# Sixteen of the 44 activation tiles of the last projection move from triple products into seven block products per pair, between its passes

## The chip, the cores and the metric

The kernel runs on one core of a Trainium2 chip. The metric is the device time of one execution in microseconds (us). TensorE (PE) multiplies, VectorE (DVE) and ScalarE (ACT) prepare and take away operands, GpSimd (POOL) and SyncE (SP) issue most of the transfers.

## What is computed

One layer of a hybrid block on 512 tokens of 2048 channels. A mixer with a modulated norm comes first, then a SwiGLU feed-forward of width 5632 and a final norm. The end is what the change is about:

```python
def _swiglu(u, w_ffn_in, w_ffn_out):
    gate, up = jnp.split(u @ w_ffn_in, 2, axis=-1)
    return (jax.nn.silu(gate) * up) @ w_ffn_out
...
        x = x + g2 * _swiglu(_modulate(_rms_norm(x, norm2_g[l]), sh2, sc2), w_ffn_in[l], w_ffn_out[l])
...
    return _rms_norm(x, norm_f_g)
```

`g2` is the last sixth of a modulation vector, `silu(c) @ w_ada + b_ada`.

## The kernel before

Everything is in fp32. Each operand is split into a high part (ACT copies it into a rounded type) and a low part (DVE subtracts), and a product is three matmuls: high by high, high by low, low by high. There is no scheduler: each engine has its program written out by hand, with counted semaphores between them, so the order within a program is fixed.

Two ways of multiplying are in use. **Triples:** a unit of 4 activation tiles (128 channels each) by 2 output tiles is 24 matmuls of 512 columns. **Block products** (`period`): for a pair of output tiles, 16 activation tiles are halved in channels and tokens, and seven half-size products (`ORDER`) with sums of weight blocks (`gate_sums`, `w_sums`) take the place of eight. Each product is 8 matmuls of 512 columns and 8 of 256. 24 periods make the merge gates, 40 make most of the feed-forward's input (`NALL` counts 64 in all). The results of the seven are combined by ACT and DVE in `up_out`, `c12_out`, `up_fold` and `gate_out`.

The last projection multiplies the 44 tiles of the hidden activation, kept in DRAM, by `w_ffn_out`. It has three passes over the activation, for output tiles 0 to 5, 6 to 11 and 12 to 15. A pass has 11 groups of 4 activation tiles, and a group has 3, 3 or 2 units. Two sets of buffers alternate: group n is loaded by SP when group n-2 has been multiplied (`b_used`), then ACT makes its high parts and DVE its low parts (`prep`: one tile `hb` of 2048 columns, and per unit one tile `bw` of 1024). At the end of a pass DVE takes the sums out of the accumulators with `down_out`, which multiplies by `g2` and adds to the rows `x1b` of the residual, and counts `b_free`. The first units of the next pass wait for `b_free`, since they write the same accumulators. ACT squares these rows and prepares them for transposing (`squares_out`), TensorE transposes them (`turn`), and `fin_evac` copies the result.

The modulation is computed on the side: chunks of `w_ada` (512 KB, 1024 columns) are loaded by POOL into a ring and added up on DVE (`chunk`, 1024 columns); then TensorE sums over partitions by one-column matmuls (`spread`). 16 chunks are added while the first projection's last 8 units run (u from 8 to 15), 64 during later stages, and the last 16, of twice the width, beside pass 0 (`chunks_late`). Their spread, of 16 columns, stands in the last group of pass 0.

## Time and profile before

| | us |
|---|---|
| median of 3 runs | 2650.99 (2649.25 to 2652.12) |
| the profiled execution, its own time | 2649.97 |
| its span from the first to the last instruction | 2648.2 |
| TensorE busy | 2609.0 (99%) |
| VectorE busy | 1891.1 (71%) |
| ScalarE busy | 1157.8 (44%) |
| last projection, first matmul | 2138.76 after the start |
| its first matmul of pass 1 / pass 2 | about 2322 / 2502 to 2508, where the passes change |

Times of places are counted from the start of the span. Busy shares say which engine has no room. Of a pipelined TensorE the distance between the starts of matmuls is the price, not the length of one. 1.8 us of the execution lie outside the span.

### The profile page before, as it was taken

What the parts mean: (1) busy time and instruction counts of PE and PEld (TensorE: products, weight loads), DVE (VectorE), ACT (ScalarE), POOL (GpSimd) and SP (SyncE); (2) the same over time, 40 slices, a digit from 0 to 9 for tenths busy, and PEclk for the clock granted to TensorE, in tenths of its full rate; (3) what the DMA queues carried; (4) which work ended last, traced back from release to release, by engine and by line L of the source; (5) the groups of instructions that cost most, each with busy time, mean ns of one, the idle gap of its engine ahead of it and who ended that gap; (6) DMA issues with size and microseconds to landing.
All of it is one profiled execution on the core that took longest, in us unless ns stands there. A gap on an engine that the chain in (4) does not pass through costs nothing.

```text
span 2648.2 us, 37757 instructions
## 1 busy us (share of the span) xinstructions
PE 2609.0 (99%) x13881; PEld 2204.5 (83%) x13881; DVE 1891.1 (71%) x2070; ACT 1157.8 (44%) x1311; POOL 175.4 (7%) x242
## 2 busy tenths in 40 slices
PE   6999999999999999999999999999999999999998
PEld 4788778878888888888788888888888888888887
DVE  4546898767999999775767878878788756533443
ACT  4214766354555555322444444444444433333333
POOL 0010000000001111110000001000010000000000
PEclk8999999999999999999999999999999999999999
DMA  9963434755556665985568888888888757644555
GB/s 369 369 198 117 137 120 147 266 175 168 162 160 168 154 163 144 330 319 193 151 160 209 202 198 203 193 210 201 195 207 196 194 207 285 246 151 158 175 178 187
DMA packets 505787, 527.43 MB, mean 199 GB/s; under 512 B 16041, under 2 KB 445937, under 8 KB 497905
## 3 DMA queue, kind: packets, MB, share of 16 engines
q1 hardware_dynamic: 464064, 388.35, 47.4%
q0 software_dynamic: 37088, 121.13, 19.0%
q10 hardware_dynamic: 4560, 16.95, 1.6%
q8 instruction: 49, 0.80, 0.1%
q14 instruction: 26, 0.21, 0.0%
HBM read 435.65 MB, written 48.76 MB: 183 GB/s over the span
## 4 chain that ended last, share of the span: by engine, by line
PE 94%; DVE 2%; ACT 1%; DMA 1%; issue 0%; ACTq 0%; DVEq 0%; SPq 0%
PE main L1549 15%; PE aux L1549 15%; PE main L1257 8%; PE main L1553 8%; PE aux L1553 8%; PE main L1258 8%; PE main L1259 8%; PE aux L1687 4%; PE aux L1688 4%; PE aux L1689 4%; PE main L1688 2%; PE main L1689 2%; PE main L1687 2%; PE aux L1432 1%; PE aux L1309 1%; DMA ada_pc<-in_w_ada 1%
## 5 line engine op out<-in xcount | busy, mean ns | idle before, releaser
L939 ACT ACTIVATE h_S<-f_S 128x1024 fp32r<-128x1024 f32 x256 | 264.2, 1057 | 385.5 <-DVE f_S L2123 186.9
L2135 DVE TENSOR_TENSOR l_S<-f_S,h_S 128x1024 fp32r<-128x1024 f32 x256 | 306.3, 1218 | 13.2 <-ACT h_S L939 13.2
L2135 DVE TENSOR_TENSOR l_A<-f_A,h_A 128x1024 fp32r<-128x1024 f32 x192 | 232.1, 1221 | 67.0 <-ACT h_A L939 56.0
L939 ACT ACTIVATE h_A<-f_A 128x1024 fp32r<-128x1024 f32 x192 | 202.3, 1057 | 133.9 <-PE aux L1553 66.0
L1810 DVE TENSOR_TENSOR w_lo<-w_raw,w_hi 128x1024 fp32r<-128x1024 f32 x120 | 145.9, 1221 | 116.6 <-ACT w_hi L733 116.3
L1257 PE MATMUL main<-u_both,w_hi 128*128 128x512 f32 x512 | 210.9, 412 | 2.5 <-DVE u_both L2330 2.5
L2420 DVE TENSOR_TENSOR hb_l<-hb_f,hb_h 128x2048 fp32r<-128x2048 f32 x33 | 75.6, 2292 | 187.4 <-ACT hb_h L1165 187.4
L733 ACT ACTIVATE w_hi<-w_raw 128x1024 fp32r<-128x1024 f32 x120 | 125.7, 1053 | 179.7 <-DMA w_raw<-in_w_out 69.5
L1687 PE MATMUL aux<-hb_h,bw_h 128*128 128x512 f32 x512 | 201.5, 394 | 0.9 <-DVE bw_l L2425 0.9
L1258 PE MATMUL main<-u_both,w_hi 128*128 128x512 f32 x512 | 201.6, 394 | 0.0
L1259 PE MATMUL main<-u_both,w_lo 128*128 128x512 f32 x512 | 200.5, 392 | 0.0
L1688 PE MATMUL aux<-hb_l,bw_h 128*128 128x512 f32 x512 | 200.3, 391 | 0.0
L1689 PE MATMUL aux<-hb_h,bw_l 128*128 128x512 f32 x512 | 200.3, 391 | 0.0
L1549 PE MATMUL main<-t_both,h_S 128*128 128x512 f32 x768 | 192.3, 392 | 0.0
L1549 PE MATMUL aux<-t_both,h_S 128*128 128x512 f32 x768 | 192.3, 392 | 0.0
L1165 ACT ACTIVATE hb_h<-hb_f 128x2048 fp32r<-128x2048 f32 x33 | 63.2, 1916 | 221.6 <-DMA hb_f<-hidden_feature_major 207.6
L1549 PEld LDWEIGHTS main<-t_both,h_S 128*128 128x128 f32 x768 | 138.2, 189 | 24.7
L1549 PEld LDWEIGHTS aux<-t_both,h_S 128*128 128x128 f32 x768 | 138.1, 189 | 24.7
L1549 PE MATMUL main<-u_both,h_A 128*128 128x512 f32 x512 | 128.2, 392 | 0.0
L1549 PE MATMUL aux<-u_both,h_A 128*128 128x512 f32 x512 | 128.2, 392 | 0.0
L1257 PEld LDWEIGHTS main<-u_both,w_hi 128*128 128x128 f32 x512 | 97.2, 190 | 30.4 <-issue 14.6
L2425 DVE TENSOR_TENSOR bw_l<-bw_f,bw_h 128x1024 fp32r<-128x1024 f32 x88 | 104.0, 1219 | 24.0 <-ACT bw_h L1170 23.8
(319 smaller groups left out, 5541.1 us busy)
## 6 DMA issues: line engine op xcount, KB each, us to landing
f_A<-in_w_ffn_in SPq DMA_DIRECT2D x120, 512.0 KB, 5.4
bw_f<-in_w_ffn_out SPq DMA_DIRECT2D x88, 512.0 KB, 6.9
f_S<-in_w_ffn_in SPq DMA_DIRECT2D x80, 512.0 KB, 4.3
f_S<-f_A POOLq DMA_DIRECT2D x80, 512.0 KB, 5.6
f_A<-in_w_in SPq DMA_DIRECT2D x72, 512.0 KB, 3.8
hb_f<-hidden_feature_major SPq DMA_DIRECT2D x33, 1024.0 KB, 4.9
w_raw<-in_w_in SPq DMA_DIRECT2D x48, 512.0 KB, 3.5
ada_pc<-in_w_ada SPq DMA_DIRECT2D x48, 512.0 KB, 7.6
```

The source lines that it names most:

```text
L733: act.activation(w_hi[:, u % RING], w_raw[:, u % RING], ACT.Copy).then_inc(hi_done, 1)
L939: act.activation(wh[v][:, :, :], wf[b][v][:, :, :], ACT.Copy).then_inc(w_hi_done, 1)
L1257: pe.matmul(dst, wh, m_hi_ap, start=start, stop=False, skip_group_check=shared)
L1258: pe.matmul(dst, wh, m_lo_ap, start=False, stop=False, skip_group_check=shared)
L1259: return pe.matmul(dst, wl, m_hi_ap, start=False, stop=stop, skip_group_check=shared)
L1549: pe.matmul(dst.rearrange("p (s n) -> p s n", n=TH), wh[v][:, k, :], moving[v](k)[0], start=start and k == 0, stop=False, skip_group_check ...
L1553: ins = pe.matmul(dst[:, low * TH:low * TH + TH], wl[b][v][:, k, :], moving[v](k)[1], start=False, stop=k == HK - 1, skip_group_check=True)
L1687: pe.matmul(dst, w_h, hb_h[b][:, cc, :], start=start and cc == 0, stop=False, skip_group_check=again)
L1688: pe.matmul(dst, w_h, hb_l[b][:, cc, :], start=False, stop=False, skip_group_check=again)
L1689: ins = pe.matmul(dst, w_l, hb_h[b][:, cc, :], start=False, stop=stop and cc == UC - 1, skip_group_check=again)
L1810: dve.tensor_tensor(w_lo[:, s], w_raw[:, s], w_hi[:, s].bitcast(F32), ALU.subtract).then_inc(lo_done, 1)
L2135: dve.tensor_tensor(wl[b][v][:, :, :], wf[b][v][:, :, :], wh[v][:, :, :].bitcast(F32), ALU.subtract).then_inc(w_lo_done, 1)
```

## The change

The 44 tiles are divided. Tiles 16 to 43 (28 tiles, 7 groups) stay with triples, in three passes as before. Tiles 0 to 15 are multiplied by block products, 8 periods for the 16 output tiles (`NALL` to `NEND`), and these periods stand between pass 0 and pass 1. The sums of pass 0 are scaled by ACT (`down_evac`) into `hidb` and added to the residual rows in DRAM by accumulating transfers of POOL. The results of the periods are scaled (`scaled`) and added in the same way. The rows are loaded only after that, with the sums in them.

During pass 0 the 16 activation tiles are loaded again (`u_f`), split, and their token sums formed on DVE (`block_token_sums`, `block_low`, `token_lo`). A third set of buffers (`SETS`) serves one group at the start. The loops of the last projection are unrolled. Half of the late chunks of `w_ada` is moved to the first projection: 32 chunks instead of 16 are added while its last 8 units run, and two spreads of 8 columns stand there where there was one. Beside pass 0, 16 chunks of 1024 columns are left, and a spread of 8 columns after group 3.

In the cut diff the lines of SP, POOL, ACT, TensorE and DVE follow each other in this order; the last loop is that of DVE over passes 1 and 2.

```diff
+EARLY_CHUNKS = {8: 5, 9: 5, 10: 5, 11: 4, 12: 4, 13: 4, 14: 3, 15: 2}
+LATE_AT = 112
...
+ND = KT // 2
+NEND = NALL + ND
-NG = NPAIR // 4
+NG = (NPAIR - KT) // 4
 LAST = 3 * NG - 1
+SETS = (0, 2, 1, 0, 1, 0, 1) + (0, 1, 0, 1, 0, 1, 0) + (1, 0, 1, 0, 1, 0, 1)
+UNITS = (3,) * NG + (3,) * NG + (2,) * NG
+G_STORED = 32 * (PW - 1)
...
+        def set_free(gg):
+
+            same = [g for g in range(gg) if SETS[g] == SETS[gg]]
+            return before(same[-1] + 1) if same else None
...
+            def group(gg):
+                if set_free(gg) is not None:
+                    sp.wait_ge(b_used, set_free(gg))
+                hidden(gg)
+                for u in range(UNITS[gg]):
+                    down(gg, u)
...
+            group(2)
+            group(3)
+            sp.wait_ge(b_used, before(2))
+            for j in range(4):
+                sp.dma_start(u_f[:, 4 * j:4 * j + 4, :], hid_fm[:, 4 * j:4 * j + 4, :]).then_inc(rows_landed[4], 16)
+            for gg in range(4, NG):
+                group(gg)
+            sp.wait_ge(b_used, before(NG - 1))
+            for v in ("S3", "A22", "A11", "A12"):
+                block_load(NALL, v)
...
+            for n in range(112, 128):
+                if n >= 116:
+                    pool.wait_ge(ada2_used, n - 3)
+                chunk(n, ada2_pl[:, n % 4, :])
+
+            pool.wait_ge(x1_stored, 128)
+            for u in range(3):
+                pool.wait_ge(b_free[u], 1)
+                pool.dma_start(x1_fm[:, 2 * u:2 * u + 2, :], hidb[:, :, :], accum_op=ALU.add).then_inc(gate_stored, 16)
+            for a in range(ND):
+                pool.wait_ge(s12_done, NALL + a + 1)
+                pool.wait_ge(gate_stored, P_STORED + 32 * a)
+                for n, src in enumerate((silu_b, up_b)):
+                    dst = x1_fm[:, 2 * a + n, :].rearrange("p (h n) -> p h n", n=TH)
+                    pool.dma_start(dst, src, accum_op=ALU.add).then_inc(gate_stored, 16)
 
...
+            def scaled(p, stored):
+
+                a = p - NALL
+                act.wait_ge(up_ready, PW + a + 1)
+                act.activation(up_b, up_b, ACT.Copy, scale=mod2[:, 49 + 2 * a:50 + 2 * a])
+                act.wait_ge(gate_ready, p + 1)
+                if stored is not None:
+                    act.wait_ge(gate_stored, stored)
+                act.activation(silu_b, spare_l[:, HK // 2:HK:2, :], ACT.Copy, scale=mod2[:, 48 + 2 * a:49 + 2 * a]).then_inc(s12_done, 1)
...
+            def down_evac(u):
+
+                if u == 0:
+                    act.wait_ge(mod2_done, 3)
+                    for b in range(2):
+                        act.wait_ge(hid_stored[b], 8 * NWIN)
+                else:
+                    act.wait_ge(gate_stored, G_STORED + 16 * u)
+                act.wait_ge(b_used, before(NG - 1) + u + 1)
+                for n in range(2):
+                    ins = act.activation(hidb[:, n, :], (aux[:, n, :], aux[:, 2 + n, :], main[:, n, :])[u], ACT.Copy,
+                                         scale=mod2[:, 48 + 2 * u + n:49 + 2 * u + n])
+                ins.then_inc(b_free[u], 1)
+            for gg in range(1, 5):
+                prep(gg)
+            act.wait_ge(rows_landed[4], 160)
+            for j in range(4):
+                act.activation(u_hi[:, 4 * j:4 * j + 4, :], u_f[:, 4 * j:4 * j + 4, :], ACT.Copy).then_inc(v_hi, 1)
+            prep(5)
+            act.wait_ge(acc_used, 8)
+            for j in range(4):
+                split_t(j, 17)
+            prep(6)
+            act.wait_ge(b_used, before(NG - 1))
+            for v in ("A11", "S2"):
+                split(NALL, NALL // 2, 0, v, True, True)
+            down_evac(0)
+            down_evac(1)
+            act.wait_ge(b_used, before(NG))
+            for v in ("S1", "A22", "A12", "S3"):
+                split(NALL, NALL // 2, 0, v, True, True)
+            for p in range(NALL, NEND):
...
-                    if u == 15:
-                        spread(0)
+                    if u in (12, 15):
+                        spread((12, 15).index(u))
...
+                    if g == 0 and ps == 2:
+                        pe.wait_ge(b_free[u], ps)
...
+                if gg == 3:
+                    pe.wait_ge(ada2_used, LATE_AT + 16)
+                    pe.wait_ge(c12_done, NALL)
+                    pe.wait_ge(c21_done, NALL)
+                    for t in range(8):
+                        ins = pe.matmul(main[:, 2, t:t + 1], ada2_al[:, t * P:t * P + P], ones[:, 0:1], start=True, stop=True)
+                    ins.then_inc(acc_used, 1)
+                if gg == NG - 1:
+                    pe.wait_ge(v_lo, KT + 4)
+                    pe.wait_ge(t_lo_done, 12)
+                    for u in range(2):
+                        pe.wait_ge(b_free[u], 1)
+                    period(NALL, 0, False)
+                    pe.wait_ge(b_free[2], 1)
+                    pe.wait_ge(mod2_done, 3)
+                    period(NALL + 1, 1, False)
+                    for p in range(NALL + 2, NEND):
+                        period(p, p % 2)
 
...
+                for n in range(done, done + EARLY_CHUNKS[u]):
+                    chunk_next(n, ada2_pa[:, n % 4, :], ada2_acc1 if n >= 16 else ada2_acc)
...
+            prep(1)
+            late(0, 4)
+            prep(2)
+            late(4, 10)
+            prep(3)
+            late(10, 16)
+            block_token_sums()
+            prep(4)
+            for j in range(4):
+                block_low(j)
+            dve.wait_ge(acc_used, 8)
+            dve.tensor_tensor(mod2[:, 56:64], main[:, 2, 0:8], prm[:, C_BADA + 88:C_BADA + 96], ALU.add).then_inc(mod2_done, 1)
+            prep(5)
+            for j in range(4):
+                token_lo(j, 9 + j)
+            prep(6)
+            dve.wait_ge(b_used, before(NG - 1))
...
+            for p in range(NALL, NEND):
+                gate_period(p, p // 2, (p + 1) // 2, p % 2, first=p == NALL, last=p == NEND - 1, merged=False,
+                            stored=P_STORED + 32 * (p - 1 - NALL) if p > NALL + 1 else None)
...
+            for gg in range(NG + 1, LAST + 1):
+                ps, g = gg // NG, gg % NG
+                if g == 2:
+                    down_out(ps - 1)
+                if g in (4, 5, 6):
+                    fin_evac(3 * ps - 3 + g - 4)
+                prep(gg)
```

The order on DVE at the change from pass 1 to pass 2, before. `hb_l` and `bw_l` are the low parts of a group, `x1b<-aux` and `x1b<-main` are `down_out`; after the two groups' preparation come three low parts that are the last group of pass 1, then the first group of pass 2.

```order
L2420 TENSOR_TENSOR hb_l_129<-hb_f_127,hb_h_131 128x2048 [waits b_hi]
L2425 TENSOR_TENSOR bw_l_142<-bw_f_141,bw_h_143 128x1024 [waits b_hi]
L2425 TENSOR_TENSOR bw_l_145<-bw_f_144,bw_h_146 128x1024 [waits b_hi]
L2425 TENSOR_TENSOR bw_l_148<-bw_f_147,bw_h_149 128x1024 [waits b_hi]
L2420 TENSOR_TENSOR hb_l_128<-hb_f_126,hb_h_130 128x2048 [waits b_hi]
L2425 TENSOR_TENSOR bw_l_133<-bw_f_132,bw_h_134 128x1024 [waits b_hi]
L2425 TENSOR_TENSOR bw_l_136<-bw_f_135,bw_h_137 128x1024 [waits b_hi]
L2460 SCALAR_TENSOR_TENSOR x1b_150<-aux,mod_194,x1b_150 128x512 [waits rows_landed0,b_used,mod2_done]
L2460 SCALAR_TENSOR_TENSOR x1b_150<-aux,mod_194,x1b_150 128x512
L2460 SCALAR_TENSOR_TENSOR x1b_151<-aux,mod_194,x1b_151 128x512 [waits rows_landed1,b_used]
L2460 SCALAR_TENSOR_TENSOR x1b_151<-aux,mod_194,x1b_151 128x512
```

The sums of pass 1 are taken out after the preparation of one group of pass 2. In the changed kernel DVE has this at the same place (the first row still belongs to the group `hb_l_130` that opens pass 2, the next `hb_l` is the second group of pass 2):

```order
L2550 TENSOR_TENSOR hb_l_130<-hb_f_129,hb_h_131 128x2048 [waits b_hi]
L2555 TENSOR_TENSOR bw_l_145<-bw_f_144,bw_h_146 128x1024 [waits b_hi]
L2555 TENSOR_TENSOR bw_l_148<-bw_f_147,bw_h_149 128x1024 [waits b_hi]
L2550 TENSOR_TENSOR hb_l_127<-hb_f_126,hb_h_128 128x2048 [waits b_hi]
L2555 TENSOR_TENSOR bw_l_136<-bw_f_135,bw_h_137 128x1024 [waits b_hi]
L2555 TENSOR_TENSOR bw_l_139<-bw_f_138,bw_h_140 128x1024 [waits b_hi]
L2641 SCALAR_TENSOR_TENSOR x1b_162<-aux,mod_207,x1b_162 128x512 [waits rows_landed0,b_used]
L2641 SCALAR_TENSOR_TENSOR x1b_162<-aux,mod_207,x1b_162 128x512
L2641 SCALAR_TENSOR_TENSOR x1b_163<-aux,mod_207,x1b_163 128x512 [waits rows_landed1,b_used]
L2641 SCALAR_TENSOR_TENSOR x1b_163<-aux,mod_207,x1b_163 128x512
```

The `x1b` rows have moved behind the preparation of the second group of pass 2. That group's set of buffers is the one that the last group of pass 1 used.

The order on DVE in pass 0, before: `ada_al` are the late chunks, `hb_l` and `bw_l` a group.

```order
L2420 TENSOR_TENSOR hb_l_129<-hb_f_127,hb_h_131 128x2048 [waits b_hi]
L2425 TENSOR_TENSOR bw_l_142<-bw_f_141,bw_h_143 128x1024 [waits b_hi]
L2425 TENSOR_TENSOR bw_l_145<-bw_f_144,bw_h_146 128x1024 [waits b_hi]
L2425 TENSOR_TENSOR bw_l_148<-bw_f_147,bw_h_149 128x1024 [waits b_hi]
L2486 SCALAR_TENSOR_TENSOR ada_al<-ada_pl,cvec,ada_al 128x1024 [waits ada2_used,ada2_landed0]
L2486 SCALAR_TENSOR_TENSOR ada_al<-ada_pl,cvec,ada_al 128x1024 [waits ada2_used]
L2486 SCALAR_TENSOR_TENSOR ada_al<-ada_pl,cvec,ada_al 128x1024 [waits ada2_used,ada2_landed1]
```

And now, from the last six chunks to the preparation of group 4 (`t_f<-u_f` are the token sums):

```order
L1948 SCALAR_TENSOR_TENSOR ada_al<-ada_pl,cvec,ada_al 128x1024 [waits ada2_used,ada2_landed2]
L1948 SCALAR_TENSOR_TENSOR ada_al<-ada_pl,cvec,ada_al 128x1024 [waits ada2_used,ada2_landed3]
L1948 SCALAR_TENSOR_TENSOR ada_al<-ada_pl,cvec,ada_al 128x1024 [waits ada2_used,ada2_landed0]
L1948 SCALAR_TENSOR_TENSOR ada_al<-ada_pl,cvec,ada_al 128x1024 [waits ada2_used,ada2_landed1]
L1948 SCALAR_TENSOR_TENSOR ada_al<-ada_pl,cvec,ada_al 128x1024 [waits ada2_used,ada2_landed2]
L1948 SCALAR_TENSOR_TENSOR ada_al<-ada_pl,cvec,ada_al 128x1024 [waits ada2_used,ada2_landed3]
L2586 TENSOR_TENSOR t_f<-u_f 128x2048 [waits rows_landed4]
L2586 TENSOR_TENSOR t_f<-u_f,t_f 128x2048 [waits t_sum]
L2586 TENSOR_TENSOR t_f<-u_f 128x2048 [waits t_sum]
L2586 TENSOR_TENSOR t_f<-u_f,t_f 128x2048 [waits t_sum]
L2550 TENSOR_TENSOR hb_l_130<-hb_f_129,hb_h_131 128x2048 [waits b_hi]
L2555 TENSOR_TENSOR bw_l_145<-bw_f_144,bw_h_146 128x1024 [waits b_hi]
```

Group 4's low parts stand behind all 16 chunks and behind four sums that wait for the reloaded activation (`rows_landed4`).

## Rows read from the trace of the kernel before

**Rows 1.** The page, part 1: busy time, share of the span, instructions.

```profile
PE 2609.0 (99%) x13881; PEld 2204.5 (83%) x13881; DVE 1891.1 (71%) x2070; ACT 1157.8 (44%) x1311; POOL 175.4 (7%) x242
```

**Rows 2.** Waits of PE (who for whom: us, times, longest), 2320 to 2649.

```profile
PE aux L1687 <- DVE bw_l L2425: 0.9, 1, 0.9
```

**Rows 3.** Timeline of PE (start, length), pass 0: a unit and the next.

```profile
2149.67 0.39 PE L1687 MATMUL main<-hb_h,bw_h 128*128 128x512 f32 x1
...
2155.11 0.39 PE L1687 MATMUL aux<-hb_h,bw_h 128*128 128x512 f32 x1
```

**Rows 4.** Timeline of PE: one product of a period and the next.

```profile
2004.69 2.00 PE L1549 MATMUL main<-t_both,h_S 128*128 128x512 f32 x8
...
2007.48 2.00 PE L1549 MATMUL main<-t_both,h_S 128*128 128x512 f32 x8
```

**Rows 5.** PE by stretches (last numbers: granted clock, DMA share, GB/s), behind the 16-column spread.

```profile
2310.00:2318.00 8.00, 8.00 (x27) 0.57 0.11 36
2312.00:2314.00 2.00, 2.00 (x6) 0.50 0.01 5
```

**Rows 6.** PE by stretches: at the restart after the second norm, and behind an 8-column spread.

```profile
1266.00:1268.00 2.00, 1.25 (x3) 0.50 0.00 0
...
1266.00:1274.00 8.00, 7.25 (x20) 0.58 0.00 1
...
219.00:221.00 2.00, 2.00 (x11) 1.00 0.96 312
```

**Rows 7.** Timeline of PE: an 8-column spread; the restart after the second norm.

```profile
217.45 1.84 PE L1348 MATMUL aux<-ones,ada_acc 128*128 128x1 f32 x16
...
1266.74 0.77 PE L1257 MATMUL main<-u_both,w_hi 128*128 128x512 f32 x1 [2.47 <-DVE u_both L2330]
```

**Rows 8.** Timeline of SP, start of pass 2: a group is loaded.

```profile
2518.45 0.34 SPq L597 DMA_DIRECT2D hb_f<-hidden_feature_major  x1
```

**Rows 9.** Timeline of ACT, the same group.

```profile
2523.37 1.92 ACT L1165 ACTIVATE hb_h<-hb_f 128x2048 fp32r<-128x2048 f32 x1 [3.44 <-DMA hb_f<-hidden_feature_major]
```

**Rows 10.** Timeline of DVE: sums of pass 1 taken out, and the same group.

```profile
2502.50 2.72 DVE L2460 SCALAR_TENSOR_TENSOR x1b<-aux,mod,x1b 128x512 f32<-128x512 f32 x4
...
2525.32 2.29 DVE L2420 TENSOR_TENSOR hb_l<-hb_f,hb_h 128x2048 fp32r<-128x2048 f32 x1 [3.41 <-ACT hb_h L1165]
2527.53 2.35 DVE L2425 TENSOR_TENSOR bw_l<-bw_f,bw_h 128x1024 fp32r<-128x1024 f32 x2
```

**Rows 11.** Timeline of DVE in pass 0: group 1's last low part, and group 3.

```profile
2154.42 1.23 DVE L2425 TENSOR_TENSOR bw_l<-bw_f,bw_h 128x1024 fp32r<-128x1024 f32 x1 [0.17 <-ACT bw_h L1170]
...
2182.15 2.29 DVE L2420 TENSOR_TENSOR hb_l<-hb_f,hb_h 128x2048 fp32r<-128x2048 f32 x1 [10.30 <-ACT hb_h L1165]
...
2187.77 4.87 DVE L2486 SCALAR_TENSOR_TENSOR ada_al<-ada_pl,cvec,ada_al 128x1024 f32<-128x1024 f32 x4
```

**Rows 12.** All engines by stretches in pass 0 (last numbers: clock, DMA share, GB/s).

```profile
2142.76:2146.76 4.00, 4.00 (x20) 3.30 (x19) 0.95 (x2) 1.92 (x1) 0.00 (x0) 1.00 1.02 417
...
2158.76:2162.76 4.00, 4.00 (x19) 3.34 (x18) 0.32 (x1) 2.27 (x2) 0.00 (x0) 1.00 1.01 361
```

**Rows 13.** The page, part 6: transfers (KB each, us to landing).

```profile
f_S<-f_A POOLq DMA_DIRECT2D x80, 512.0 KB, 5.6
...
ada_pw<-in_w_ada POOLq DMA_DIRECT2D x48, 512.0 KB, 6.3
...
mixed_feature_major<-u_hi_spare POOLq DMA_DIRECT2D x46, 256.0 KB, 4.8
```

**Rows 14.** Groups by line from 2130 on: ACT's scaled copy.

```profile
L1205 ACT ACTIVATE x_fin<-x1b,prm 128x512 f32<-128x512 f32 x12 | 7.9, 708 | 0.0
```

**Rows 15.** Transfers of the early chunks: us to landing.

```profile
DMA to landing us min/median/max: 3.7/5.4/8.5
```

**Rows 16.** Timeline of DVE, first projection: first chunks; end of its last unit.

```profile
153.60 0.75 DVE L1816 TENSOR_SCALAR ada_acc<-ada_pa,cvec 128x1024 f32<-128x1024 f32 x1
...
217.65 0.69 DVE L1925 COPY pad<-aux 128x512 f32<-128x512 f32 x1 [8.51 <-PE aux L1259]
```

More of the change, by code:

```diff
@@ L344, in half_ready @@
             if gates:
-                eng.wait_ge(gate_added, p * 2 + (1, 2)[v == "S3"])
+                first = 2 * NWIN if isinstance(p, int) and p >= NALL else 0
+                eng.wait_ge(gate_added, p * 2 + ((1, 2)[v == "S3"] - first))
             else:
@@ new lines, in _ @@
+            sp.wait_ge(product_done, 7 * (PW + p) + 1)
+            hid_store(p - 1, p // 2 - 1, 1)
+            sp.wait_ge(product_done, 7 * (PW + p) + 3)
+            down(0, 0)
+            sp.wait_ge(product_done, 7 * (PW + p) + 5)
+            for pr in range(2):
+                sp.wait_ge(hid0_stored[pr], 16)
+            hidden(0)
+            p = NWIN - 1
+            sp.wait_ge(product_done, 7 * (PW + p) + 1)
+            hid_store(p - 1, p // 2, 0)
+            down(0, 2)
+            sp.wait_ge(product_done, 7 * (PW + p) + 2)
@@ new lines, in _ @@
+            for v in ("S3", "A22", "A11", "A12"):
+                block_load(NALL, v)
+            block_load(NALL + 1, "A11")
+            for n, v in enumerate(("A12", "S3", "A22")):
+                sp.wait_ge(b_used, before(NG - 1) + n + 1)
+                block_load(NALL + 1, v)
+            for p in range(NALL, NEND):
+                ahead = p + 2 < NEND
+                sp.wait_ge(product_done, p * 7 + 1)
+                if ahead:
+                    block_load(p + 2, "A11")
+                if p == NEND - 1:
+                    down(NG, 2)
+                    sp.wait_ge(product_done, p * 7 + 2)
+                    down(NG, 1)
+                if p == NEND - 2:
+                    sp.wait_ge(product_done, p * 7 + 3)
+                    down(NG, 0)
+                    sp.wait_ge(product_done, p * 7 + 5)
+                    hidden(NG)
+                for n, v in ((4, "A22"), (5, "A12"), (6, "S3")):
+                    if ahead:
+                        sp.wait_ge(product_done, p * 7 + n)
+                        block_load(p + 2, v)
@@ L656, in _ @@
+            sp.wait_ge(product_done, 7 * NEND)
+            sp.wait_ge(c21_done, NEND)
+            group(NG + 1)
+            sp.wait_ge(s12_done, NEND)
+            sp.wait_ge(gate_stored, P_STORED + 32 * ND)
+            x1_load(0, 3)
+            for gg in range(NG + 2, LAST + 1):
+                if gg in (2 * NG - 1, LAST):
+                    x1_load(3 * (gg // NG), UNITS[gg])
+                group(gg)
             for t in range(4):
@@ L1183, in first_down @@
                 elif step == 1:
-                    act.wait_ge(product_done, 7 * NALL - 6)
-                    down_hi(0, 0, 1)
-                    act.wait_ge(product_done, 7 * NALL - 4)
-                    down_hi(0, 0, 2)
-            period(NALL - 1, NALL // 2 - 1, None, 1, last=True, extra=first_down)
+                    act.wait_ge(product_done, 7 * end - 6)
+                    down_hi(gg, 1)
+                    act.wait_ge(product_done, 7 * end - 4)
+                    down_hi(gg, 2)
@@ L1524, in _ @@
             pe.wait_ge(four_lo_done, 4)
-            spread(2)
+            spread(3)
             for n in range(8):
@@ L1933, in _ @@
                 lo(0, 8, 0, u + 2)
-                chunks_early(2 * u - 16, 2 * u - 15)
+                done = sum(EARLY_CHUNKS[v] for v in range(8, u))
+                for n in range(done, done + EARLY_CHUNKS[u]):
+                    chunk_next(n, ada2_pa[:, n % 4, :], ada2_acc1 if n >= 16 else ada2_acc)
                 if u % 4 == 3:
@@ L2181, in gate_period @@
                     gate_sums(p + 1, cn, 1 - b, "S1")
-                if not first:
+                if not first and merged:
                     merge(p - 1)
@@ new lines, in block_low, with late @@
+            def block_low(j):
+                dve.wait_ge(v_hi, KT + j + 1)
+                dve.wait_ge(t_sum, 17)
+                rows = slice(4 * j, 4 * j + 4)
+                dve.tensor_tensor(u_lo[:, rows, :], u_f[:, rows, :], u_hi[:, rows, :].bitcast(F32), ALU.subtract).then_inc(v_lo, 1)
+            def late(first, end):
+                for n in range(LATE_AT + first, LATE_AT + end):
+                    chunk_next(n, ada2_pl[:, n % 4, :], ada2_al)
+            prep(1)
+            late(0, 4)
```

417 lines of the change are left out of this document (185 added, 232 removed).

## The prediction

> **What bounds the kernel now.** Part 1 of the page comes first: TensorE is busy for 99% of the span, no other engine over 71% [rows 1]. So only two things can move the end: how long TensorE's own matmuls take, and gaps that open between them. The waits of TensorE say that the last projection has one gap, 0.9 us at the start of pass 2, for a low part from DVE [rows 2]; the chain of waits there runs through `down_out`, the squares and the preparation of the next group. Next come prices at TensorE. A unit of triples starts 5.44 us after the one before it (2155.11 - 2149.67) [rows 3], which is 24 matmuls at 0.2267. A product of a period starts 2.79 us after the one before it (2007.48 - 2004.69) [rows 4], 7 of them make a period of 19.55 us. Last, the granted clock: behind the 16-column spread of pass 0 it falls to 0.50, that is from 2.4 to 1.2 GHz. A mean of 0.57 over 8 us means 6.9 us at half speed ((1 - 0.57) x 2 x 8) [rows 5], so 3.4 us lost. Behind an 8-column spread (1.8 us) it stays at 1.00 [rows 6, 7].
>
> **TensorE's own work.** 4 groups of 8 units leave: 32 x 5.44 = 174.1 us. 8 periods come: 8 x 19.55 = 156.4 us. Gain 17.7 us. The 16 spread columns are now 8 and 8, the same total. The transposes and the tail stay. The Trainium skill (TensorE: Matmul & The Clock Gate, Back-to-back issue gap) gives N / 2.4 + 2.5 ns for one isolated matmul at the full clock, 215.8 ns for 512 columns and 109.2 ns for 256. By it a unit is 5.18 us and a period 18.2 us, and the gain 165.7 - 145.6 = 20.1 us. The rows above are of the very two patterns, and they decide.
>
> **Gap at the start of pass 2.** This is the costliest edit, and it is in the order of DVE's program. Before, the sums of pass 1 are taken out behind the preparation of one group of pass 2. Now they stand behind two. The second of these groups (number 15) uses the buffers of group 13, the last of pass 1, so SP loads it only when group 13 is done. TensorE's next unit (group 14) waits for `b_free`, which `down_out` counts. So a ring closes: end of pass 1, load, high part, low part, `down_out`, and only then TensorE. Its length stands in the rows of a group with the same two units: load issued at 2518.45 [rows 8], high part begins 2523.37 [rows 9], low parts end 2529.88 (2527.53 + 2.35) [rows 10], 11.4 us after the issue. Then two of the `x1b` operations, a half of 2.72 us, 1.4 [rows 10]. TensorE stands still for 12.8 us. The second unit follows in time, since 1.4 is less than a unit. Such a gap also costs clock. The nearest row is the restart after the second norm, behind idle time and one-column matmuls: it begins at 1266.74 [rows 7], where the clock is 0.50, and the mean of 0.58 from 1266 to 1274 [rows 6] puts its return at 1272.7 ((1 - 0.58) x 2 x 8 = 6.7 us). 6 us at half speed, 3.0 us lost. Nothing below zero is open here; above, 3.4 us as in [rows 5]. The old gap of 0.9 us in this place goes [rows 2], since the preparation of group 15 is done before. Term: 12.8 + 3.0 - 0.9 = +14.9.
>
> **From pass 0 into the periods.** The first period writes the accumulators of units 0 and 1. ACT has to scale both out into `hidb`, which holds one unit, and the second waits until the first has been added in DRAM. Counted from the end of group 5 (E): the four weight blocks are loaded at E, and sums and high parts S1 and S2 come first in ACT's order. With about 3.5 us to the first landing and 1.4 for each further block of 0.52 MB at some 385 GB/s (between the rates in [rows 12]), A11 has landed at E + 6.3; DVE's sums of 1.2 us each (half of the 2.35 in [rows 10]) reach `S2` at E + 8.8; ACT's high part of it ends at E + 9.9. Two scaled copies at 0.7 us [rows 14] end at E + 11.3. The accumulating transfer: no row has 512 KB into DRAM. 256 KB into DRAM land after 4.8 us, 512 KB accumulated into a buffer on the chip after 5.6 [rows 13]. I take 6. Then 1.4 for the next two copies: E + 18.8. TensorE wants to begin at E + 16.3. Gap 2.5 us. Bounds: 0 if the transfer takes 3.5 us, 6 if it takes 9.5. The Trainium skill (DMA: Bandwidth & Descriptors, Anatomy of one DMA) has 2.0 us plus bytes over 436 GB/s for a transfer from GpSimd, 3.2 us here. By that estimate the gap would be zero and the total 2.5 us less. The third evacuation lies inside the first period. What waits behind ACT's wait are the high parts of the third and later products, needed 5.6 us after the start; two of ACT's operations fit in, so they are in time.
>
> **The periods themselves.** They are gate periods without the multiplication of the branch, so DVE has less to do than in the 24 that run without a gap now. Cover: 19.55 us of TensorE each. If it failed it would do so eight times; rival 4 has that. The entry into pass 1 is the old entry into pass 0, which shows no wait. The residual rows are loaded later (after the last accumulation), 10 us into pass 1 at the latest, and needed only by `squares_out` before group 9: hidden by 32 us of multiplying.
>
> **DVE's queue in pass 0.** Group 4 is wanted 4 x 16.3 + 2.0 = 67.3 us after the first matmul of the projection (2138.76). In front of it on DVE, from 16.9 on, where group 1's low parts end as now (2154.42 + 1.23) [rows 11]: 16 chunks at 1.22 = 19.5 (a fourth of 4.87), two groups at 5.6 = 11.2 (2187.77 - 2182.15), four sums over 2048 columns at 2.3 = 9.2 (as the `hb_l` of 2.29) [rows 11], and 3.5 for group 4's first two low parts: 43.4, so 60.3 if it never waits. It waits for transfers: until the reloaded activation is there, 20.7 MB must move (three groups 7.9, 16 chunks 8.4, activation 4.2, a store 0.3). At 361 to 417 GB/s [rows 12] that takes 50 to 57 us. Then 9.2 + 3.5: group 4 is ready between 62 and 70, at most 2.7 us late by the rows' rates, and up to 7 if DVE's ring of chunks and the queue of groups hinder each other. Group 5 comes at 84.0 against 85.2 wanted, group 6 at 99 against 101.5: in time. Against a lateness stands a gain: the 16-column spread is gone, and if TensorE goes on at once behind 8 columns, the clock stays up (+3.4). If group 4 is late by 2 us or more, 1.8 us of spread and the idle together are as long as the stretch that cost the clock before, and nothing is gained. Together between -3.4 and +7. I take 0, a little late or a half of the gain.
>
> **Early chunks.** 32 instead of 16 chunks are added on DVE while its last 8 units run, with a ring of four. The first four have landed and end at 158.0 (153.60 + 0.75 [rows 16] + 3 x 1.22). The other 28 go at (landing + 1.22 + 0.3 for the issue) / 4 each: with 5.4 us [rows 15] 1.73, with 8.5 us 2.5; 6.3 us, as `ada_pw` has under load [rows 13], 1.96. The last ends at 206, 228, or 213. The second spread is asked for at 219.5 (217.65 [rows 16] plus the first spread). The likely case costs nothing; the bound is 8.6 us.
>
> **Sum.** -17.7 + 14.9 + 2.5 + 0 + 0 = -0.3 us. Against the profiled execution's own 2649.97 (span 2648.2 and 1.8 outside) that is 2649.7; the median of the runs lies 1.0 above it, so 2650.7 for a run. Forecast: **2650.5 us**. A gain of TensorE is eaten by one wait.
>
> **Rivals.**
> 1. The wait at pass 2 does not bind, or the group is loaded far sooner than 4.9 us. Against it: the order is fixed and `b_used` is waited for before the load. Then -17.7 - 0.9 + 2.5: 2635.
> 2. DVE is late in pass 0: group 4 by 7 us or more. For it: the reload starts only at 33 us behind group 3 in SP's queue, and chunks share the transfer engines. From 70.5 us on it costs more than my sum holds. 2650.5 + 7 to 10: 2658 to 2661, slower.
> 3. The early chunks are late: landing over 7 us on average decides. The second spread, and `conv` behind it on DVE, come late. +8.6: 2659.
> 4. The accumulations into DRAM hold the periods up: `up_fold` waits for the pair before. Now two accumulations of 256 KB take 4.8 us of 19.55, which speaks against. If each period lost 1.5 us: +12, 2662.
>
> **Chances.** The forecast 60% (2644 to 2656), rival 1 8%, rival 2 13%, rival 3 11%, rival 4 8%. A measurement of this kernel tells about 0.2%, 5.3 us, from no change. Faster by more: rival 1 and a tenth of the forecast's share and a little (no gap into the periods and the clock kept), 0.17. Slower by more: the rest of the rivals and two points of the forecast's, 0.32. Same: 0.51. Range 2642 to 2661: the lower end is -0.3 - 2.5 - 3.4 - 2 for a cheaper restart, the upper that of rivals 2 and 3; about 2 in 10 stay outside.
>
> **What would show it.** Units and products at the same distances. TensorE idle 12 to 14 us before the first matmul of group 14, released by DVE's `x1b`, with the clock at 0.50 behind it; two to three us idle before the first product of the periods, released by ACT; at most 3 us before group 4, released by DVE's low part; none before the second early spread. The prediction is wrong if the gap at pass 2 is under 9 or over 16 us, or if the engine waits inside the periods.

## The result, and the profile after

The changed kernel takes 2661.14 us (median of 6 runs, 2657.38 to 2664.2), the kernel before 2649.02 (6 runs). The ratio is 1.0043, interval 1.003 to 1.0056: slower by 0.4%. The forecast was 2650.5, in a range whose upper end, 2661.0, lies just below. The profiled execution took 2659.25 us of its own (span 2657.5), 9.3 more than the one of before, while the medians lie 12.1 apart. What follows accounts for the profiled pair.

Page, part 1, after; it answers to [rows 1]:

```profile
PE 2595.8 (98%) x14009; PEld 2202.8 (83%) x14009; DVE 1988.1 (75%) x2176; ACT 1199.0 (45%) x1377; POOL 205.5 (8%) x277
```

TensorE works less and the span is longer, so the time is in gaps. The waits of TensorE in the last projection, after (us in total, times, longest), where [rows 2] had one of 0.9:

```profile
PE aux L1811 <- DVE x1b L2641: 12.8, 1, 12.8
PE aux L1811 <- DVE bw_l L2555: 7.1, 2, 3.8
PE aux L1672 <- ACT hidb L1293: 3.6, 1, 3.6
PE main L1824 <- DVE out_tm L2654: 0.6, 1, 0.6
```

The last one lies in the tail, where before has none. Where the other four waits stand, in the timeline of TensorE (start, length, idle before and releaser): before group 1, before group 4, before the first block product, before group 14.

```profile
2159.58 0.65 PE L1811 MATMUL aux<-hb_h,bw_h 128*128 128x512 f32 x1 [3.76 <-DVE bw_l L2555]
...
2215.40 0.80 PE L1811 MATMUL aux<-hb_h,bw_h 128*128 128x512 f32 x1 [3.29 <-DVE bw_l L2555]
...
2270.98 1.39 PE L1672 MATMUL aux<-u_both,h_A 128*128 128x512 f32 x5 [3.62 <-ACT hidb L1293]
...
2558.96 0.80 PE L1811 MATMUL aux<-hb_h,bw_h 128*128 128x512 f32 x1 [12.76 <-DVE x1b L2641]
```

And TensorE by stretches around each of the four, after (length, busy, then granted clock, DMA share, GB/s), to be read as [rows 5] and [rows 6]:

```profile
2158.00:2164.00 6.00, 4.42 (x12) 0.72 1.06 378
2214.00:2222.00 8.00, 6.60 (x17) 0.57 0.66 225
2270.00:2278.00 8.00, 7.02 (x31) 0.79 0.67 142
2558.00:2564.00 6.00, 5.04 (x15) 0.62 0.01 3
```

Each mean clock gives the time at half speed: with a mean of 0.72 over 6 us it is (1 - 0.72) x 2 x 6 = 3.4 us. What of it lies before the first matmul of the stretch costs nothing, since TensorE stands idle then. Half of the rest is lost: 1.7 us, 2.9 (6.9 at half speed, 1.0 of them idle), 1.7, and 1.8 (4.6, 1.0 idle). Together 8.1.

The profiles, experiments included, reach the last projection's first matmul at 2138.8 to 2143.0 us, with the same program up to there but for the chunks and their spreads. So I compare below what lies between that matmul and the end of the span. Before: 2648.2 - 2138.76 = 509.4. After: 2657.5 - 2139.31 = 518.2. One piece of work has left this stretch: its spread had 16 columns before and has 8 now, the other 8 stand in the first projection. Before, then after:

```profile
2307.43 4.16 PE L1736 MATMUL main<-ones,ada_al 128*128 128x1 f32 x32
```

```profile
2210.27 1.84 PE L1853 MATMUL main<-ones,ada_al 128*128 128x1 f32 x16
```

At the full clock 16 columns take 3.6 us (the row of f_spread below), so 1.8 us are gone from the stretch; the 4.16 hold a part of the old fall of the clock. The account: 509.4 - 17.7 of work - 1.8 of spread + 24.0 of idle time + 8.1 of clock - 0.9 (old gap) - 3.4 (the fall behind the 16-column spread, which is gone) = 517.7; 0.5 stay unexplained.

**The ring at pass 2, as it ran.** SP, ACT and DVE around it, after, to be read beside [rows 8 to 10]:

```profile
2546.23 0.34 SPq L630 DMA_DIRECT2D hb_f<-hidden_feature_major  x1
...
2551.08 1.91 ACT L1253 ACTIVATE hb_h<-hb_f 128x2048 fp32r<-128x2048 f32 x1 [12.23 <-DMA hb_f<-hidden_feature_major]
...
2553.02 2.29 DVE L2550 TENSOR_TENSOR hb_l<-hb_f,hb_h 128x2048 fp32r<-128x2048 f32 x1 [11.64 <-ACT hb_h L1253]
2555.23 2.35 DVE L2555 TENSOR_TENSOR bw_l<-bw_f,bw_h 128x1024 fp32r<-128x1024 f32 x2
2557.50 2.72 DVE L2641 SCALAR_TENSOR_TENSOR x1b<-aux,mod,x1b 128x512 f32<-128x512 f32 x4
```

The load goes out as group 13 ends, the sums are taken out 11.3 us later, and TensorE starts behind the first two of them.

### The profile page after: what moved, and what is told of

The parts are those of the page before. It is cut to its first block, busy times and chain, and to the rows that moved or that the text cites. A ratio compares the mean times of both kernels' runs of the same rounds, so it can differ in the third digit from the quotient of the medians.

```text
span 2657.5 us, 38062 instructions
## 1 busy us (share of the span) xinstructions
PE 2595.8 (98%) x14009; PEld 2202.8 (83%) x14009; DVE 1988.1 (75%) x2176; ACT 1199.0 (45%) x1377; POOL 205.5 (8%) x277
## 4 chain that ended last, share of the span: by engine, by line
PE 90%; DVE 4%; DMA 2%; ACT 1%; issue 1%; ACTq 0%; SPq 0%; DVEq 0%; POOLq 0%
PE aux L1672 17%; PE main L1672 17%; PE aux L1676 9%; PE main L1676 9%; PE main L1379 8%; PE main L1380 8%; PE main L1381 8%; PE aux L1811 2%; PE aux L1812 2%; PE aux L1813 2%; PE aux L1555 1%; PE aux L1431 1%; PE aux L1380 1%; PE aux L1381 1%; PE aux L1379 1%
## 5 line engine op out<-in xcount | busy, mean ns | idle before, releaser
L1013 ACT ACTIVATE h_S<-f_S 128x1024 fp32r<-128x1024 f32 x288 | 297.3, 1057 | 427.0 <-DVE f_S L2252 206.8
L2264 DVE TENSOR_TENSOR l_S<-f_S,h_S 128x1024 fp32r<-128x1024 f32 x288 | 344.9, 1219 | 21.2 <-ACT h_S L1013 21.2
L2264 DVE TENSOR_TENSOR l_A<-f_A,h_A 128x1024 fp32r<-128x1024 f32 x216 | 261.0, 1221 | 73.5 <-ACT h_A L1013 53.3
L1811 PE MATMUL aux<-hb_h,bw_h 128*128 128x512 f32 x320 | 128.1, 400 | 19.8 <-DVE x1b L2641 12.8
L2550 DVE TENSOR_TENSOR hb_l<-hb_f,hb_h 128x2048 fp32r<-128x2048 f32 x21 | 48.1, 2290 | 116.9 <-ACT hb_h L1253 116.9
L1812 PE MATMUL aux<-hb_l,bw_h 128*128 128x512 f32 x320 | 127.0, 397 | 0.0
L1813 PE MATMUL aux<-hb_h,bw_l 128*128 128x512 f32 x320 | 126.6, 396 | 0.0
L1676 PEld LDWEIGHTS aux<-t_both,l_S 128*128 128x128 f32 x864 | 117.9, 190 | 8.4
L1676 PEld LDWEIGHTS main<-t_both,l_S 128*128 128x128 f32 x864 | 117.9, 190 | 8.4
L1672 PEld LDWEIGHTS aux<-u_both,h_A 128*128 128x128 f32 x576 | 103.9, 189 | 22.6 <-issue 4.0
```

The costliest lines, as they stand in the source:

```text
L1013: act.activation(wh[v][:, :, :], wf[b][v][:, :, :], ACT.Copy).then_inc(w_hi_done, 1)
L1672: pe.matmul(dst.rearrange("p (s n) -> p s n", n=TH), wh[v][:, k, :], moving[v](k)[0], start=start and k == 0, stop=False, skip_group_check ...
L1676: ins = pe.matmul(dst[:, low * TH:low * TH + TH], wl[b][v][:, k, :], moving[v](k)[1], start=False, stop=k == HK - 1, skip_group_check=True)
L1811: pe.matmul(dst, w_h, hb_h[b][:, cc, :], start=start and cc == 0, stop=False, skip_group_check=again)
L1812: pe.matmul(dst, w_h, hb_l[b][:, cc, :], start=False, stop=False, skip_group_check=again)
L1813: ins = pe.matmul(dst, w_l, hb_h[b][:, cc, :], start=False, stop=stop and cc == UC - 1, skip_group_check=again)
```

## Experiments

"From the first matmul" is the stretch just defined, from each profile; medians and ratios are against the kernel before on the same chip.

| kernel | median (before there) | ratio, interval | from the first matmul |
|---|---|---|---|
| before | | | 509.4 |
| after | 2661.14 (2649.02) | 1.0043, 1.003 to 1.0056 | 518.2 |
| b_order | 2661.74 (2648.43) | 1.0055, 1.0038 to 1.0072 | 519.8 |
| e1_undo | 2648.72 (2648.43) | 1.0001, 0.9991 to 1.001 | 506.2 |
| e1b_split | 2646.35 (2649.90) | 0.9987, 0.9977 to 0.9996 | 505.4 |
| e2_count | 2658.41 (2648.43) | 1.0036, 1.0022 to 1.005 | 514.3 |
| e3_prep4 | 2661.50 (2648.43) | 1.0050, 1.0033 to 1.0066 | 518.6 |
| e3b_order | 2655.16 (2649.90) | 1.0021, 1.0012 to 1.003 | 511.9 |
| e4_buf | 2658.29 (2649.90) | 1.0030, 1.0019 to 1.0041 | 513.7 |
| all_four | 2631.57 (2649.90) | 0.9929, 0.9916 to 0.9943 | 486.8 |
| all_four_again | 2628.69 (2649.48) | 0.9918, 0.9903 to 0.9933 | 486.7 |
| f_spread | 2632.80 (2649.48) | 0.9934, 0.992 to 0.9948 | 489.5 |
| f_reload | 2661.98 (2649.48) | 1.0046, 1.0031 to 1.0062 | 520.1 |

### The order at pass 2, undone and done alone

e1_undo, DVE's loop (ACT's has the same change in front of `squares_out`):

```diff
-                if g == 2:
+                if g == (2, 1)[ps - 1]:
                     down_out(ps - 1)
```

> The changed kernel, with down_out(1) and squares_out(3) put back in front of the preparation of the second group of pass 2. Theory (the order on DVE closes the ring): the idle 12.8 us before the first matmul of group 14 goes to under 1 us, and the clock behind it stays at 1.00 (1.8 us were lost); 2661.1 - 12.8 - 1.8 + 1 gives about 2647.5. Rival (the gap only moves): group 15 is prepared behind the squares and is late itself; TensorE then idles 3 to 5 us after group 14 and loses clock there, 2652. Rival (the order is no cause, the load is late anyway): the gap stays over 9 us, 2660.

b_order, in the kernel before, on ACT and on DVE:

```diff
-                    if ps and g == 1:
+                    if ps and g == ps:
                         down_out(ps - 1)
```

> The kernel before, with one thing of the change: the sums of pass 1 are taken out behind the preparation of two groups of pass 2, not one (down_out(1) and squares_out(3)). Theory: TensorE idles 12.8 us before group 22 and loses 1.8 us of clock, the old 0.9 us goes: 2649.0 + 13.7 = 2662.7. Rival (it takes the rest of the change too): under 1 us more, 2650.

Both came as the theory of the order has it. e1_undo gave 2648.72, 0.3 above the kernel before on its chip where the changed kernel is 12.1 above, and the 12.8 us are gone. Its timeline of TensorE shows what is left of the ring, before group 15:

```profile
2561.16 0.50 PE L1811 MATMUL aux<-hb_h,bw_h 128*128 128x512 f32 x1 [1.81 <-DVE bw_l L2555]
```

The waits of TensorE in b_order, from 2130 on, are this row alone:

```profile
PE aux L1687 <- DVE x1b L2460: 12.9, 1, 12.9
```

So this order alone costs a kernel without any block product in its last projection 13.3 us in the medians. In its trace it is 10.4, because the clock did not fall behind the spread in that profile (see f_spread): 12.9 + 1.9 of clock - 0.9 - 3.4 = 10.5.

e1b_split asks what the 1.8 us in e1_undo wait for. In DVE's `down_out` the part that counts `b_free` stands in front of group 15's preparation, the addition of squares and ACT's `squares_out` stay behind it:

```diff
+                if ps == 2 and g == 1:
+                    down_out(1)
                 if g == 2:
-                    down_out(ps - 1)
+                    squares_added(ps - 1)
```

> The changed kernel; in pass 2 only the evacuation of the sums (b_free) stands in front of the preparation of the second group, squares and their addition stay behind it. The whole down_out and squares_out in front left 1.8 us of idle before group 15's first unit. Theory (squares on ACT held group 15's high parts): with the squares behind, group 15 is ready at 11.4 + 0, TensorE idles under 1 us there, 2647. Rival (the load and preparation of group 15, 11.4 us against 10.9 of multiplying, are the limit whatever stands in front): 1 to 2 us of idle stay, 2648.5.

No wait is left in pass 2, and 2646.35 came out: the squares on ACT had held the high parts of group 15. Of the rival, that 11.4 us of preparation are more than the 10.9 of a group, nothing shows: TensorE did not idle.

### Group 1: one count for four loads

```diff
-            if SETS[gg] == 2:
-                eng.wait_ge(rows_landed[3], 80 + 64)
+            if SETS[gg] == 2:
+                if u is None:
+                    eng.wait_ge(rows_landed[3], 80 + 16)
+                else:
+                    eng.wait_ge(bw_landed[6 + u], (128, 128, 208)[u] + 16)
```

(`bw_landed[6:9]` are three semaphores whose earlier use has ended, with their final counts. The rest of the edit names them and lets the loads count on them.)

> The changed kernel, with four semaphores for the four loads of group 1 (set 2) in place of one shared count of 64. Theory (the count): the high part of hb waits now for its own load alone and begins near 2147 in place of 2154.15; group 1's first unit is ready before 2155.8, the 3.8 us of idle and 1.7 us of clock go, 2661.1 - 5.5 = 2655.6. Rival (traffic: groups 2 and 3 and four chunks of w_ada share the transfer engines): hb and the first bw land after 2151 each, the gap stays at 2 to 4 us, 2659 to 2661.

ACT's high part of group 1, in the changed kernel:

```profile
2154.15 1.92 ACT L1253 ACTIVATE hb_h<-hb_f 128x2048 fp32r<-128x2048 f32 x1 [11.42 <-DMA bw_f<-in_w_ffn_out]
```

and in e2_count:

```profile
2147.46 1.92 ACT L1255 ACTIVATE hb_h<-hb_f 128x2048 fp32r<-128x2048 f32 x1 [1.71 <-DMA hb_f<-hidden_feature_major]
```

Counted from the first matmul that is 14.8 and 5.1 us. The count was the cause: a high part of `hb` that names a load of `bw` as its releaser. The wait before group 1 is gone. But the kernel gained 2.1 us in the medians (12.1 above the kernel before, now 10.0) and 3.9 from the first matmul, not 5.5, since the wait before group 4 grew from 3.3 to 5.8:

```profile
2215.25 0.79 PE L1813 MATMUL aux<-hb_h,bw_h 128*128 128x512 f32 x1 [5.77 <-DVE bw_l L2557]
```

TensorE came to group 4 5.7 us sooner after its first matmul, group 4 was ready only 3.2 sooner (72.9 for 76.1). The expectation had missed that: the first gap had hidden a part of the second. And the 3.2 us say that the count made group 4 late as well: DVE begins the first late chunk 16.9 us after the first matmul here and 22.4 in the changed kernel, and the four buffers of chunks are filled again only behind DVE.

### Group 4: DVE's order in pass 0

e3_prep4 moves `prep(4)` in front of `block_token_sums()`. e3b_order does that too and goes further; its edit against the changed kernel:

```diff
-            block_token_sums()
             prep(4)
-            for j in range(4):
-                block_low(j)
+            block_token_sums()
             dve.wait_ge(acc_used, 8)
             dve.tensor_tensor(mod2[:, 56:64], main[:, 2, 0:8], prm[:, C_BADA + 88:C_BADA + 96], ALU.add).then_inc(mod2_done, 1)
             prep(5)
             for j in range(4):
-                token_lo(j, 9 + j)
+                block_low(j)
+            token_lo(0, 9)
             prep(6)
+            for j in range(1, 4):
+                token_lo(j, 9 + j)
```

> The changed kernel, with group 4's preparation on DVE in front of the four token sums. Theory (DVE's order holds group 4): the 3.3 us before group 4 go, with 2.9 us of clock. But group 5 stands behind four sums (9.2) and four low parts (8.9) then: ready near 2231.5 where TensorE wants it at 2228.4, so a gap of about 3 us opens there, and the total is 2661.1 - 6.2 + 3 + 2 = 2660. Rival (DVE has room): group 5 is in time, 2655. Rival (the load of group 4 is what is late): the gap before group 4 stays over 2 us.

> The changed kernel; on DVE group 4 is prepared before the token sums, group 5 before the low parts of the reloaded activation, group 6 before three of the four low parts of the token sums. Theory (the order holds groups 4 and 5): no wait in pass 0 but that before group 1, 3.3 of idle and 2.9 of clock go: 2655. Rival (pass 0 is held by transfers, not by the order): group 4 or 5 stays over 2 us late, 2659. Rival (the first period is reached before its operands): a new wait of over 1 us before the first product, with DVE as releaser.

The gap moved by one group in e3_prep4, as worked out, and the time stayed (2661.50; 518.6 us from the first matmul for 518.2). Its timeline of TensorE:

```profile
2234.54 0.80 PE L1811 MATMUL aux<-hb_h,bw_h 128*128 128x512 f32 x1 [3.82 <-DVE bw_l L2555]
```

e3b_order has no wait in pass 0 but that before group 1, and took 2655.16, 6.3 us less than the changed kernel from the first matmul. Its last chunk is added no sooner (begun 63.1 us after the first matmul, 62.2 in the changed kernel). So the order is what let late chunks hold TensorE: the work that is wanted last stood first.

f_reload tests the other half, that the transfers set when DVE comes to group 4. SP loads two pieces again (the two waits for the activation, on ACT and on DVE, are raised with it, from 160 to 192):

```diff
-            for j in range(4):
+            for m, j in enumerate((0, 1, 2, 3, 0, 1)):
+                if m == 4:
+                    sp.wait_ge(rows_landed[4], 160)
```

> The changed kernel, with two of the four pieces of the reloaded activation (1.05 MB each) loaded a second time, once the four have landed; the token sums wait for these too. It moves 2.1 MB more in front of the last chunks and changes nothing else. Theory (until the last late chunk is there the transfers are the limit, 23 MB at some 370 GB/s): the last chunk and group 4 behind it come 2.1 / 0.37 = 5.7 us later, the gap before group 4 goes from 3.3 to 9 us, 2667. Rival (DVE's own queue is the limit, transfers have room): the gap stays at 3 to 4 us, 2661.

The gap before group 4 went from 3.3 to 5.75 us, 2.4 more, between what the theory and the rival had. The run does not price what it was to price. SP waited with the two pieces, and so issued group 4's load at 2200.44, behind them and not in front of the last chunks. DVE in f_reload:

```profile
2206.90 2.29 DVE L2588 TENSOR_TENSOR t_f<-u_f 128x2048 f32<-128x2048 f32 x1 [4.11 <-DMA u_f<-hidden_feature_major]
```

It shows that DVE waits for a transfer there, and no more than that. The median (2661.98) can't be told from that of the changed kernel.

### The entry into the block products: a second buffer

`down_evac(1)` writes into the free rows of `silu_b` and `up_b`, and POOL adds from there in two transfers. Of the edit, ACT's wait:

```diff
-                else:
-                    act.wait_ge(gate_stored, G_STORED + 16 * u)
+                elif u == 1:
+                    act.wait_ge(v_lo, KT + 4)
+                else:
+                    act.wait_ge(gate_stored, G_STORED + 48)
```

> The changed kernel; the second evacuation of pass 0 goes into the free rows of silu_b and up_b, so it doesn't wait for the first one's accumulation in DRAM. Theory (the single buffer holds the entry): the 3.6 us before the first product go, with 1.7 us of clock: 2655.8. Rival (weight sums and high parts are late as well): 1 to 3 us of idle stay, releaser DVE or ACT's high part, 2658.

The wait is gone and the clock stays at 1.00. From the first matmul 4.5 us were saved, which is 3.6 + 1.7, less 0.9 by which the gap before group 4 was longer in this profile (4.2 for 3.3). The medians say 3.7 (12.1 above the kernel before, now 8.4). High parts and weight sums were in time.

### All four, and the columns of the spread

all_four joins e1b_split, e2_count, e3b_order and e4_buf. f_spread repeats its 8 columns:

```diff
-                    for t in range(8):
+                    for t in (0, 1, 2, 3, 4, 5, 6, 7) * 2:
```

> All four mendings together (evacuation first in pass 2, four counters for group 1, DVE's order in pass 0, second buffer at the entry). Theory (each wait is a fault of order or buffer, the work alone is worth -17.7 us): 2649.0 - 17.7, plus 1 us before group 4 (ready near 2207.5, wanted at 2206.6 now that group 1 is in time) and up to 1.5 us of clock behind it: 2632 to 2634. Rival (transfers of pass 0 are the limit: 23 MB have to move until the last of the chunks is added): group 4 and the stream behind it stay 3 us or more late, 2637 to 2640.

> The kernel with all four mendings, in which the 8-column spread behind group 3 is issued twice, so 16 one-column matmuls pairs of columns stand together as in the kernel before (the numbers stay the same). Theory of the forecast (16 columns cost the clock 3.4 us, 8 don't): 2631.6 + 1.8 for the columns + 3.4 = 2636.8, with the clock at 0.50 behind them. Rival (the fall behind 16 columns is not tied to their number; the kernel with only the order changed showed none behind its 16): 2633.4, the clock stays at 1.00.

> The kernel with all four mendings on the same chip as the doubled spread, for the difference of the two: 2631.6, no wait of TensorE in the last projection but in its tail.

all_four beats both kernels: 2631.57 and, on another chip, 2628.69, ratios 0.9929 and 0.9918. The wait of up to 1 us before group 4 that was expected did not show. Its waits of TensorE, from 2130 on, are one row in the tail:

```profile
PE main L1837 <- DVE out_tm L2668: 0.8, 2, 0.6
```

f_spread took 4.1 us more than all_four_again on the same chip (profiles: 2.8 from the first matmul). The columns themselves are 1.8 of that. The clock is 1.7, less than the 3.4 of before, and all_four_again has 0.8 of waits in its tail that f_spread has not: 1.8 + 1.7 - 0.8 = 2.7 in the profiles. f_spread's timeline of TensorE, and the stretch around the spread with two pieces behind it:

```profile
2208.28 3.62 PE L1866 MATMUL main<-ones,ada_al 128*128 128x1 f32 x32
```

```profile
2208.00:2216.00 8.00, 8.00 (x46) 0.79 0.83 284
2212.00:2214.00 2.00, 2.00 (x6) 0.51 0.98 365
2214.00:2216.00 2.00, 2.00 (x8) 0.64 1.10 368
```

all_four_again, behind its 8 columns, which end at 2208.35:

```profile
2206.00:2214.00 8.00, 8.00 (x44) 1.00 0.81 269
```

But b_order, whose 16 columns end at 2312.38, has:

```profile
2308.00:2316.00 8.00, 8.00 (x53) 1.00 0.57 190
2316.00:2324.00 8.00, 8.00 (x37) 1.00 0.00 0
```

So behind 3.6 us of one-column matmuls the clock fell in two profiles of three (before, f_spread), and behind 1.8 us of them with no stop after them in none: in neither profile of all_four, nor in [rows 6]. In the clock, halving the spread is a gain of 0 to 3.4 us.

## Why the prediction was wrong

- **TensorE's own work, -17.7: right.** In the changed kernel a unit still starts 5.44 us after the one before (2188.51 and 2193.95), and a product 2.79 after:

```profile
2300.55 2.00 PE L1672 MATMUL main<-t_both,h_A 128*128 128x512 f32 x8
2302.39 1.11 PE L1676 MATMUL main<-t_both,l_A 128*128 128x256 f32 x8
2303.34 2.00 PE L1672 MATMUL main<-u_both,h_A 128*128 128x512 f32 x8
```

  With the four waits gone, all_four is 22.6 us shorter than before from the first matmul. Less the old gap (0.9), the fall of the clock (3.4) and the eight columns that left the stretch (1.8), and with its 0.8 us of waits in the tail added, that is 17.3. f_spread, with the 16 columns of before, a fall of 1.7 and no tail wait, gives the same: 19.9 - 0.9 - 1.7. It is near the rows' 17.7 and not the 20.1 that the forecast had worked out with the Trainium skill (TensorE: Matmul & The Clock Gate, Back-to-back issue gap).
- **Gap at pass 2, +14.9: right.** Idle time 12.76 for 12.8. The clock took 1.8 for 3.0, since it was back 3.6 us after the restart, not 6. e1_undo and b_order show the cause.
- **Into the periods, +2.5: mechanism right, mis-sized.** It was 3.6 us of idle time and 1.7 of clock, and e4_buf took both away. The two pairs of scaled copies on ACT, after:

```profile
2262.16 1.25 ACT L1293 ACTIVATE hidb<-aux,mod 128x512 f32<-128x512 f32 x2
2269.46 1.27 ACT L1293 ACTIVATE hidb<-aux,mod 128x512 f32<-128x512 f32 x2 [6.06 <-DMA x_feature_major<-hidb]
```

  TensorE wanted to begin at 2267.4 (2270.98 - 3.62), 16.3 after the end of group 5, so E is 2251.1, and the first pair ends at E + 12.3 for the 11.3 forecast: weights and sums were 1 us later than counted. The accumulation took the 6 us that were estimated, from the end of one pair to the start of the next. The tile `hidb`, its transfers in the changed kernel:

```profile
DMA to landing us min/median/max: 5.3/5.4/5.6
```

  The estimate of 3.2 us by the Trainium skill (DMA: Bandwidth & Descriptors, Anatomy of one DMA) was short of it by 2.2. What the term left out is the clock behind the gap, 1.7 us: the forecast had priced a fall behind the long gap, and before group 4 as a gain that is lost, but not here.
- **DVE's queue in pass 0, taken as 0: wrong. This is the step that failed, twice.** It stood for group 1 in time, group 4 a little late or half of the clock's gain kept; the runs show 3.8 + 1.7 before group 1 and 3.3 + 2.9 before group 4, less 3.4 for the old fall of the clock: +8.3.
  First, "where group 1's low parts end as now". DVE, after:

```profile
2158.31 3.49 DVE L2555 TENSOR_TENSOR bw_l<-bw_f,bw_h 128x1024 fp32r<-128x1024 f32 x3
```

  They end at 2161.80, not at 2155.65 [rows 11], which is 5.6 us later when the start (0.55 later) is taken off. `group_landed` has the engines wait for 80 + 64 where the set is 2, that is for all four loads of the group, and I had not held that against the rows. The third set of buffers was costed at nothing, with no cover named. It cost 3.8 + 1.7, and e2_count, which changes the count alone, takes the wait away.

  Second, "group 4 is ready between 62 and 70". It was ready at 76.1 (2215.40 - 2139.31). The rows of DVE, after:

```profile
2201.55 1.28 DVE L1948 SCALAR_TENSOR_TENSOR ada_al<-ada_pl,cvec,ada_al 128x1024 f32<-128x1024 f32 x1 [2.22 <-DMA ada_pl<-in_w_ada]
2202.75 2.28 DVE L2586 TENSOR_TENSOR t_f<-u_f 128x2048 f32<-128x2048 f32 x1
...
2211.93 2.29 DVE L2550 TENSOR_TENSOR hb_l<-hb_f,hb_h 128x2048 fp32r<-128x2048 f32 x1
```

  The sums and first low parts took 9.2 + 3.5, as counted. What came late is their start: 63.4 us after the first matmul, not 50 to 57, with the last chunk. The 20.7 MB left out the 2.6 MB of group 4's own load, which SP issued at 2194.14, while DVE was still waiting for chunks; and all engines by stretches (last numbers: clock, DMA share, GB/s) show that the rate fell for 10 us. Little was asked for then: SP issued no load from 2162.2 to 2177.8, and POOL waited 6.1 us, until 2173.8, for DVE to free a buffer of the ring.

```profile
2160.00:2170.00 10.00, 10.00 (x39) 8.13 (x38) 9.66 (x9) 6.59 (x6) 2.13 (x4) 0.84 1.06 381
2170.00:2180.00 10.00, 10.00 (x46) 8.29 (x45) 8.92 (x8) 2.12 (x2) 2.65 (x5) 1.00 0.77 260
2180.00:2190.00 10.00, 10.00 (x46) 8.29 (x45) 9.05 (x7) 0.00 (x0) 1.41 (x3) 1.00 0.99 385
```

  From 2140 to 2200 the mean of six such rows is 362 GB/s, 21.7 MB. Of the 8.8 us of lateness (76.1 against the 67.3 at which group 4 was wanted) 3.2 go with the count of group 1, as e2_count shows. In its profile and the three of all_four and f_spread the last chunk is begun 58.7 to 59.2 us after the first matmul, in the six profiles that keep the count and load nothing more 62.2 to 63.9. How the rest is divided between the load of group 4 and the ring was not taken apart. That DVE's order made TensorE pay for it is shown by e3b_order. The 8.8 us cost only 3.3 + 2.9, since 5.5 of them were hidden by the wait before group 1.
- **Early chunks, 0: right.** The last one ends before its spread begins, by 3.3 us (DVE, then TensorE, after):

```profile
212.62 2.67 DVE L1948 SCALAR_TENSOR_TENSOR ada_acc<-ada_pa,cvec,ada_acc 128x1024 f32<-128x1024 f32 x2
```

```profile
218.57 1.84 PE L1471 MATMUL aux<-ones,ada_acc 128*128 128x1 f32 x16
```

- **The rivals.** Of rival 2 (13%) the condition came true, group 4 late by 7 us or more. That its 2658 to 2661 is near the measured 2661.1 is luck: group 4's lateness cost 6.2 us, not 7 to 10, and the rest is the wait before group 1, which no case had, and the larger price of the entry. Rivals 1, 3 and 4 did not show: the wait at pass 2 binds, the early chunks are in time, and TensorE has no wait inside the eight periods.

The sum again with what was measured: -17.7 + 12.8 + 1.8 - 0.9 (pass 2) + 3.6 + 1.7 (entry) + 3.8 + 1.7 (group 1) + 3.3 + 2.9 (group 4) - 3.4 + 0.6 (tail) = 10.2, where the forecast had -0.3. The profiled executions lie 9.3 apart, the medians 12.1. The forecast's chances do not add up as told: rivals 2 to 4 and two points more are 34%, not 32%; nothing hangs on it.

## What to carry to other kernels

When an edit adds a set of buffers, look at what each engine waits for before it touches it: one count over several loads makes the first user wait for the last load. When DVE's program is refilled, write behind each item when it is wanted, and put the item that TensorE wants first in front; and count every transfer that is issued before the awaited one lands, the next group's too. Two latenesses in a row are not a sum: here mending the first alone gave back 3.9 of the 5.5 us that its rows say.
